# Attention weights and convolution columns transposed by 32x32 blocks on VectorE and carried by ScalarE, in a two-block fp32 network on one Trainium2 core

## What is computed

```python
# every attention kind ends in
s = einsum('bhqd,bhkd->bhqk', q, k) * scale       # masked per kind
p = softmax(s, axis=-1)                           # or stick-breaking weights
o = einsum('bhqk,bhkd->bhqd', p, v)
# layers 0, 1: y = concat(o_a, o_b, o_m) * silu(gate); x = x + y @ w_out
# layers 2, 3: y_b = conformer_conv(ub) * silu(zb)  (a * sigmoid(gt), 31-tap causal
#              depthwise convolution over time, layer norm, silu), then
# x = x + (g0 * (y_a @ w_a) + g1 * (y_b @ w_b) + g2 * (y_c @ w_c)) @ w_out
```

## Time and profile before

| what | value |
|---|---|
| median of 3 runs | 3073.47 us (3073.46 to 3076.04) |
| time of the profiled execution | 3073.5 us |
| its span, first to last instruction | 3071.7 us |
| PE busy, weight loads | 3050.2 us (99%), 2554.8 us (83%) |
| DVE busy | 2058.9 us (67%) |
| ACT busy | 1987.5 us (65%) |
| TensorE clock granted | 0.999 of full speed |

### The profile page before, as it was taken

How to read it: one execution, slowest core, us unless ns; L and a number is a source line. 1 busy time by engine, 2 the same in 40 slices (tenths; PEclk the granted TensorE clock), 3 DMA queues, 4 the chain that set the end, 5 groups by cost and what they waited for, 6 DMA issues and landing times. The chain is left out here.

```text
span 3071.7 us, 37627 instructions
## 1 busy us (share of the span) xinstructions
PE 3050.2 (99%) x14252; PEld 2554.8 (83%) x14252; DVE 2058.9 (67%) x3042; ACT 1987.5 (65%) x3213; POOL 7.7 (0%) x20
## 2 busy tenths in 40 slices
PE   8999999999999999999999999999999999999998
PEld 7888888888888888888888888888888888888886
DVE  6555565566556799998655555659998975555564
ACT  7677677678668457687744445764668785444553
POOL 0000000000000000000000000000000000000000
PEclk9999999999999999999999999999999999999999
DMA  8556665655556665556566666666565656666664
GB/s 303 181 162 178 179 200 173 209 158 165 178 185 193 187 185 176 167 174 178 178 191 192 193 194 193 192 192 188 160 198 159 179 175 183 195 207 193 192 193 150
DMA packets 306309, 570.24 MB, mean 186 GB/s; under 512 B 18352, under 2 KB 45136, under 8 KB 305744
## 3 DMA queue, kind: packets, MB, share of 16 engines
q1 hardware_dynamic: 302240, 557.65, 60.4%
q10 hardware_dynamic: 3040, 6.42, 0.6%
q0 software_dynamic: 848, 3.76, 0.4%
HBM read 565.66 MB, written 2.10 MB: 185 GB/s over the span
## 5 line engine op out<-in xcount | busy, mean ns | idle before, releaser
L137 DVE TENSOR_TENSOR wl<-raw,wh 128x1024 fp32r<-128x1024 f32 (+2 forms) x1072 | 1282.8, 1202 | 799.0 <-ACT wh L126 795.2
L126 ACT ACTIVATE wh<-raw 128x1024 fp32r<-128x1024 f32 (+2 forms) x1072 | 1113.1, 1044 | 887.0 <-PE gp L111 863.5
L111 PE MATMUL gp<-wh,Hh 128*128 128x512 f32 (+2 forms) x2336 | 910.2, 390 | 0.0
L111 PE MATMUL gp<-wh,Hl 128*128 128x512 f32 (+2 forms) x2336 | 898.9, 385 | 0.0
L111 PE MATMUL gp<-wl,Hh 128*128 128x512 f32 (+2 forms) x2336 | 898.7, 385 | 0.0
L111 PE MATMUL gp<-wh,Yh 128*128 128x512 f32 (+3 forms) x1952 | 760.1, 389 | 8.6 <-DVE wl L137 8.6
L111 PE MATMUL gp<-wh,Yl 128*128 128x512 f32 (+3 forms) x1952 | 753.9, 386 | 0.0
L111 PE MATMUL gp<-wl,Yh 128*128 128x512 f32 (+3 forms) x1952 | 753.8, 386 | 0.0
L111 PEld LDWEIGHTS gp<-wh,Hl 128*128 128x128 f32 x2336 | 438.7, 188 | 87.8
L111 PEld LDWEIGHTS gp<-wh,Hh 128*128 128x128 f32 x2336 | 438.9, 188 | 85.2 <-issue 1.0
L111 PEld LDWEIGHTS gp<-wl,Hh 128*128 128x128 f32 x2336 | 439.1, 188 | 83.9
(11 more groups left out here) (138 smaller groups left out, 1260.1 us busy)
## 6 DMA issues: line engine op xcount, KB each, us to landing
raw<-in_w_in SPq DMA_DIRECT2D x544, 512.0 KB, 3.7
raw<-in_ev_w_in SPq DMA_DIRECT2D x104, 512.0 KB, 3.8
raw<-in_od_w_in SPq DMA_DIRECT2D x80, 512.0 KB, 3.8
raw<-in_w_out SPq DMA_DIRECT2D x64, 512.0 KB, 4.8
raw<-in_ev_w_out SPq DMA_DIRECT2D x40, 512.0 KB, 4.3
raw<-in_od_w_out SPq DMA_DIRECT2D x36, 512.0 KB, 4.5
raw<-in_w_b_out SPq DMA_DIRECT2D x32, 512.0 KB, 4.5
raw<-in_w_a_out SPq DMA_DIRECT2D x32, 512.0 KB, 4.9
```

The lines of the kernel that those rows point to most:

```text
L111: return self.e.matmul(out, l, r, start=start, stop=stop)
L126: return self.e.activation(out, in_, func, **kw)
L137: return self.sketch(157 + size(a) * 1.042) if self.e is None else self.e.tensor_tensor(out, a, b, op)
```

## The change

For the groups with `flipped` set (all but 4, 7, 8 and 9: 64 heads with 384 keys and three transposes each) the PE transposes `ptr`/`sptr` and the copies `pcopy`/`spcopy` go. In their place DVE's `flip_p` transposes a head's weights by 32x32 blocks within `tmp`, and for each pair of heads ACT's `move_p` carries both in 4 steps of 4 activates (32 partitions, 2 x 3 x 32 elements) into the place in `G` where the pair's queries and keys stood, which its scores have used up; for this, queries and keys of a head now stand side by side in most groups. `pv` reads its weights there. It now serves the stick groups too.

`glu_turn`/`glu_copy` and `zb_turn` give way to `flip_glu`/`glu_move` and `flip_zb`/`zb_move`, with 16 activates each for four halves. `zb` is carried into `k` and `v` of region 0, so `zb_move` waits for the outputs of the first stick group; the two `zb` GEMMs stand ahead of the last `silu` GEMM of the second stick group. After the roots of four norms a step `load_tanh` loads another table, which has Tanh and the exponential. `rope` is cut in two steps for the planner.

```diff
+EXP_TANH = "exp_and_others"
@@ Lane.tables
-            self.e.preload_act_table_set(LN_EXP)
+            self.e.preload_act_table_set(LN_EXP if func == ACT.Ln else EXP_TANH)
@@ Group.__init__
-        self.carried = True
+        self.carried = self.flipped = True
+        self.side_by_side = kind in ("mla", "moba", "stick") or kind == "dil" and heads == 4
@@ Program.tables
+        for g in (4, 7, 8, 9):
+            self.groups[g].flipped = False
...
+                if g:
+                    self.zb.append([gemm(L, "H", 0, W, C["zb"] + 512 * hb, 512, 16, "zb", None, hb) for hb in range(2)])
                 gr.gate = gemm(L, "H", 0, W, C["zc"] + 512 * g, 512, 16, "silu", gr.gid)
-            self.zb.append([gemm(L, "H", 0, W, C["zb"] + 512 * hb, 512, 16, "zb", None, hb) for hb in range(2)])
@@ Program
+    def turned_weights(self, gid, j):
+        gr = self.groups[gid]
+        r, n = self.region[gr.region], sum(self.keys(gr))
+        if gr.side_by_side:
+            return r["qk"][:, 2 * j:2 * j + 2, 0:n], None
+        at = {"swa": 1024 + 768 * (j % 2), "mem": 1024 + 1024 * j, "dil": 1024, "dsa": 1280 + 1024 * j}[gr.kind]
+        last = self.p_o.at((gid, 2 * j - 4), (gid, 2 * j - 3)) if j >= 2 else None
+        return r["all"][:, at:at + 2 * n].rearrange("p (h c) -> p h c", c=n), last
@@ pe_program
     def pv(gid, h):
...
-        e.wait_ge(*P.a_p.at((gid, h)))
+        if gr.flipped:
+            e.wait_ge(*P.a_pmove.at(*((gid, h // 2, a) for a in range(4))))
+            s = P.turned_weights(gid, h // 2)[0][:, h % 2, :]
+        else:
+            e.wait_ge(*P.a_p.at((gid, h)))
+            s = P.tmp.buf((gid, h))
...
-    def sptr(gid, h):
...
-    def sav(gid, h):
...
-    def glu_turn(l, hb, i):
...
-    def zb_turn(l, hb, i):
...
@@ act_program
+    def load_tanh(name):
+        e.behind("root", name)
+        e.tables(ACT.Tanh)
...
-    def spcopy(gid, h):
...
+    def move_p(gid, j, a):
+        x = P.weights(gid, j)
+        y, last = P.turned_weights(gid, j)
+        e.wait_ge(*P.v_pflip.at((gid, 2 * j), (gid, 2 * j + 1)))
...
+        for b in range(4):
+            u = x[32 * a:32 * a + 32].rearrange("p h (c b r) -> p h c b r", b=4, r=32)
+            v = y[32 * b:32 * b + 32].rearrange("p h (c a r) -> p h c a r", a=4, r=32)
+            i = e.activation(v[:, :, :, a, :], u[:, :, :, b, :], ACT.Copy)
+        i.then_inc(*P.a_pmove.up((gid, j, a)))
...
-    def glu_copy(l, hb, i):
...
+    def glu_move(l, hb, a):
...
+        carry(P.nat.buf(g), P.cv[:, 4 * hb:4 * hb + 4, :], a).then_inc(*P.a_glu.up((l, hb, a)))
...
+    def zb_move(l, hb, a):
+        g = P.zb[l][hb].g
+        e.wait_ge(*P.v_zflip.at((l, hb)))
+        e.wait_ge(*P.v_y.at(*((12 + 4 * l, h) for h in range(4))))
...
+        carry(P.nat.buf(g), P.region[0]["kv"[hb]], a).then_inc(*P.a_zmove.up((l, hb, a)))
@@ dve_program
+    def flip_p(gid, h):
+        gr = P.groups[gid]
+        s = P.tmp.buf(P.score_name(gid, h))[:, 0:sum(P.keys(gr))]
+        e.wait_ge(*(P.v_a.at((gid, h)) if gr.kind == "stick" else P.a_exp.at((gid, h, "end"))))
+        e.flip(s, s).then_inc(*P.v_pflip.up((gid, h)))
@@ add_steps
+        if name in ("kv", "x1", "x2", "x3"):
+            add("act", "load_tanh", name)
...
+            add("dve", "flip_p", gr.gid, h)
+            if h % 2:
+                for a in range(4):
+                    add("act", "move_p", gr.gid, h // 2, a)
+                for i in (h - 1, h):
+                    add("pe", "pv", gr.gid, i)
+                    add("dve", "stick_out" if gr.kind == "stick" else "head_out", gr.gid, i)
```

More of the change, by code:

```diff
@@ L817, in heads, with score_name, weights @@
             return [(col(r["q"], h), col(r["q"], 2 + h))]
-        return [(col(r["q"], h), col(r["k"], h))]
+    def score_name(self, gid, h):
+        return ("a", gid, h) if self.groups[gid].kind == "stick" else (gid, h)
+    def weights(self, gid, j):
+        a, b = (self.tmp.which.get(self.score_name(gid, 2 * j + i), i) for i in range(2))
+        n = sum(self.keys(self.groups[gid]))
+        s = slice(a, b + 1, b - a) if a < b else slice(a, b - 1 if b else None, b - a)
+        return self.scores[:, s, 0:n]
+    def turned_weights(self, gid, j):
+        gr = self.groups[gid]
+        r, n = self.region[gr.region], sum(self.keys(gr))
+        if gr.side_by_side:
+            return r["qk"][:, 2 * j:2 * j + 2, 0:n], None
+        at = {"swa": 1024 + 768 * (j % 2), "mem": 1024 + 1024 * j, "dil": 1024, "dsa": 1280 + 1024 * j}[gr.kind]
+        last = self.p_o.at((gid, 2 * j - 4), (gid, 2 * j - 3)) if j >= 2 else None
+        return r["all"][:, at:at + 2 * n].rearrange("p (h c) -> p h c", c=n), last
     def values(self, gr, h, i):
@@ L1081, in pv @@
         m.then_inc(*P.p_o.up((gid, h)))
-        P.tmp.give((gid, h), P.p_o, (gid, h))
+        if not gr.flipped:
+            P.tmp.give((gid, h), P.p_o, (gid, h))
     def zs(gid, h):
@@ L1462, in pcopy @@
         P.bank.give(("p", gid, h), P.a_p, (gid, h))
-    def spcopy(gid, h):
-        e.wait_ge(*P.p_p.at((gid, h)))
-        e.activation(P.tmp.buf(("a", gid, h))[:, 0:384], P.bank.buf(("p", gid, h))[:, 0:384],
-                     ACT.Copy).then_inc(*P.a_p.up((gid, h)))
-        P.bank.give(("p", gid, h), P.a_p, (gid, h))
+    def move_p(gid, j, a):
+        x = P.weights(gid, j)
+        y, last = P.turned_weights(gid, j)
+        e.wait_ge(*P.v_pflip.at((gid, 2 * j), (gid, 2 * j + 1)))
+        if a:
+            e.behind("move_p", gid, j, a - 1)
+        elif last:
+            e.wait_ge(*last)
+        for b in range(4):
[3 more added lines that the diff above has]
+        i.then_inc(*P.a_pmove.up((gid, j, a)))
+        if a == 3:
+            for h in (2 * j, 2 * j + 1):
+                P.tmp.give(P.score_name(gid, h), P.a_pmove, (gid, j, a))
     def softplus(gid, h):
@@ L1617, in refine, with rope @@
         P.st.give(name, P.v_rs, name)
-    def rope(g, u):
+    def rope(g, u, part):
         gm = P.gemms[g]
         view, cos, sin, half, H, step = gm.rope
-        P.tmp.take(("r", g, u))
-        e.wait_ge(*(P.s_tab2 if gm.L >= 2 else P.s_tab).at("t"))
-        e.wait_ge(*P.a_evac.at((g, "end")))
-        if u:
-            e.behind("rope", g, u - 1)
-        e.wait_ge(*P.tmp.free(("r", g, u)))
+        if part:
+            e.behind("rope", g, u, 0)
+        else:
+            P.tmp.take(("r", g, u))
+            e.wait_ge(*(P.s_tab2 if gm.L >= 2 else P.s_tab).at("t"))
+            e.wait_ge(*P.a_evac.at((g, "end")))
+            if u:
+                e.behind("rope", g, u - 1, 1)
+            e.wait_ge(*P.tmp.free(("r", g, u)))
         buf = P.tmp.buf(("r", g, u))
@@ L1851, in tap @@
                 if not i:
[L1852 removed]
+                    e.wait_ge(*P.a_glu.at(*((l, c0 // 4, a) for a in range(4))))
                     e.wait_ge(*P.g_pad.at(l))
@@ L2212, in add_steps @@
             l, hb = gm.L - 2, gm.part
+            add("dve", "flip_zb", l, hb)
+            for a in range(4):
+                add("act", "zb_move", l, hb, a)
             for i in (0, 2):
-                add("pe", "zb_turn", l, hb, i)
                 add("dve", "zb", l, hb, i)
```

149 lines of the change are left out of this document (74 added, 75 removed).

## The result

The change takes 30 us off: the median of 4 runs is 3043.37 us (3043.09 to 3043.91) against 3073.47 for the kernel before (3073.27 to 3076.04, 4 runs beside them). The ratio is 0.9901, 95% interval 0.9888 to 0.9914. The forecast of 3046.5 has the right sign and nearly the right size, but the range began at 3043.5, 0.13 us above what came. The profiled execution took 3043.26 us, its span is 30.2 us shorter, and what follows is told of it.

The account below looks back on a forecast made before the run. PE was taken to bound the kernel, with ACT's and DVE's added work hidden beside it. 3073.5 us, less 28.6 for transposes and interruptions, plus 1.6 given back, made 3046.5 us; range 3043.5 to 3056.5.

Parts of the forecast that it names:

- PE bounds the kernel; what it no longer does comes off.: Whole kernel: PE busy 3050.2 of 3071.7 us, so removed PE work shortens the time if feeding engines keep up.
- The transposes are 256 x 0.107 = 27.4 us.: On PE: 256 removed transposes, each priced at 0.107 us by distance between starts, save 27.4 us.
- 46 x 0.026 = 1.2 us: On PE: 102 interruptions of the fills in place of 148, at 0.026 us each, save 1.2 us.
- The low end: Range's lower limit, 3043.5 us: 30.0 us off, at 0.115 to 0.117 a transpose with its interruption share, nothing given back.
- I take 1.6 us, near the lower end: Dense attention pieces, fills 464 to 479, layer 3, 256 to 271: PE loses 1.6 us of a possible 8.8.
- The last group of layers 0 and 1 keeps its old way, so the output projections there wait as before.: Output projections of layers 0 and 1: no new wait, since their last group is left unchanged.
- ACT and DVE: Whole kernel: ACT gains 221 us to about 2208, DVE 45 us to about 2,100, both beside PE's work.
- Rival 2, ACT becomes the bound: Attention stretches: slower, past 3079.6 us, if `move_p` activates cost 0.57 us each in place of 0.374; chance 0.03.
- its sum of slack: Four attention stretches: ACT's slack of 31.1, 18.8, 11.6 and 5.0 us, together 66.5 us, under PE's time.
- Rivals 3 and 4: PE transposes: 3, nothing comes of it, 3067 to 3079 us, chance 0.05; 4, whole duration counts, 3003 us, chance 0.01.

Follow-up runs that it names:

- The experiment with equal work: Changed kernel with 96 unused transposes at fills 560 to 655: one after each fill, 3057.08 us; eight after every eighth fill, 3054.03 us.
- e_dead_same_order: Changed kernel with 192 unused PE transposes put back ahead of the flipped heads' `pv`, hidden from the planner so the order stays: 3064.93 us.
- e_unflip3: Changed kernel with group 3, ahead of layer 0's memory group, back at PE's transposes (12 more): 3043.40 us.
- e_moves_by_head: Changed kernel with each `move_p` activate split in two, one for each head (1,024 of 96 elements for 512 of 192), planned anew: 3115.70 us.
- e_all_flipped: Changed kernel with groups 4, 7, 8 and 9 turned by the new way too, 50 PE transposes fewer: 3078.23 us, ratio to before 1.0015.
- e_zb_last: Changed kernel with the two `zb` GEMMs back behind the last `silu` GEMM: 3082.80 us, ratio to before 1.0031.
- the last two kernels: Changed kernel without the four early table loads (`load_tanh`), 3044.07 us; changed kernel with `rope` as one step again, 3045.13 us.
- the one pair of runs that parts the two: Changed kernel with 192 unused transposes put back: order planned anew, 3067.24 us; hidden from the planner with the order kept, 3064.93 us.

## Why the prediction was nearly right, and where it was wrong

- **PE bounds the kernel; what it no longer does comes off.** Right: 30.2 us of span for 31.4 of PE's busy time, and 0.112 a transpose when they are put back with the order kept (distances alone 0.109).
- **"The transposes are 256 x 0.107 = 27.4 us."** Right within 2%: 0.109, 27.9 us.
- **"46 x 0.026 = 1.2 us" for the interruptions.** This is the step that failed, by its size. It read the distance up to the second matmul of the next fill and took the rest of the fill for undisturbed. The traces show 3.6 us. The experiment with equal work gives 0.036 a place, so 46 fewer places are 1.7 us of it. The rest is a part that the step didn't have at all: the 102 places that stay are cheaper once most hold no transposes, and `e_dead_same_order`, which puts them back there, costs 1.7 us beyond the distances. With 2.4 us more here and 0.5 in the transposes, and 0.4 of small things, saved time is 31.9 and not 28.6.
- **The low end.** 3043.5 was 30.0 saved and nothing given back. Its 30.0 took the dearer of two readings of the transposes and had nothing beside it for the fills behind them. With the 31.9 that were saved and nothing given back it would have been 3041.6.
- **Given back: "I take 1.6 us, near the lower end".** The size came out, 1.7, but by luck: half of it is a wait of the start that I don't put down to the change, and the other half lies elsewhere than I looked. In fills 464 to 479, where ACT was reckoned to need 50.9 us against PE's 47.4, it needs 51.5 against 46.9, so the reckoning was right and the loss was not: a lead of 9.8 us covered it, and 5.2 were left.
- **"The last group of layers 0 and 1 keeps its old way, so the output projections there wait as before."** Wrong, by 0.86 us at fill 148. The last group does, but ACT is behind from group 3, and `e_unflip3` removes the wait.
- **ACT and DVE.** Right: 361 ns for `G<-tmp`; 2196.0 us against 2208, where the gaps between activates were counted and the page's busy time leaves them out; DVE 2094.6 against 2104. Tables cost nothing that a wait shows. 13,996 PE instructions, ends of 8.5 and 13.2 us.
- **Rival 2, ACT becomes the bound, 0.03.** It didn't come, but the change stood nearer to it than its sum of slack said. It let ACT take 66.5 us more in attention before PE would pay anything; in `e_moves_by_head` ACT does 55 more, in another order, and PE pays 72. In `e_all_flipped` and `e_zb_last` too the time went at a few places where a projection needed the last result of the chain, which no slack of a stretch tells. Two parts of the change that I priced at nothing or not at all are each worth more than the whole gain: four groups left out (+34.9 without) and the `zb` GEMMs' earlier place (+39.4 without).
- **Rivals 3 and 4** fell: the distances of transposes are the price, not 272 ns each, and they did come off.

Open: what part of the 0.7 and 1.8 us of the last two kernels is the step's own; what part of the 72 us of `e_moves_by_head` is its order; and why up to half of the distances behind an interruption are 2 to 4% longer.

## What to carry to other kernels

Where PE is the bound, price what is removed by distances between starts and follow them until they are the usual ones again, a whole fill behind the place. Where work moves to an engine with room, look not at its average but at the hand-offs: what is the last thing that the next projection needs, how many steps of the fuller engine stand ahead of it, and which buffer do they hold; 208 us more of ACT's work were hidden here, and 10 to 16 lost at a single wait in the kernels that did a little more. With a planner, keep the order when you test a price: an order planned anew cost 2.3 us by itself in the one pair of runs that parts the two, and where it isn't kept the experiment can't say what the work alone costs.

## What the runs showed of the hardware that was not expected

- In fills of 512 columns matmuls start 227 ns apart. In the fill behind short fp32 matmuls, 37% of the distances (49% in the kernel before) are 230 to 236 ns; in all other fills of the changed kernel 46 of 10,932 are. A PSUM read of ACT or DVE beside a matmul is not enough for it: outside the fills behind interruptions 29 of 1,121 distances with such a read were long, and 17 of 9,811 without. The cause is not shown.
- A wait of 11 us costs more than itself: the granted clock was 0.50 from 443.8 to 457.4, and matmuls stood about twice as far apart until it was back.
- An activate on 32 partitions takes 272, 361 and 415 ns for 96, 192 and 256 elements, which is 0.9 ns an element and a fixed part of about 185 ns. The duration is not the price: those of 96 elements overlap and start 0.23 us apart (eight in 1.86 us), those of 192 start 0.37 apart (four in 1.47 us in the changed kernel), so that a move cut in two costs about a quarter more and not half as much again. In busy time it is 231.8 us for 184.9.
